# Softmax normalisation by eight pairs of ScalarE activations instead of two VectorE products

## What is computed

```python
s = jnp.einsum("bnqkgd,bnskd->bnkgqs", qb, kb) * (HEAD_DIM ** -0.5)
s = jnp.where(mask[None, :, None, None, :, :], s, NEG_INF)
m = jnp.maximum(jnp.max(s, axis=-1, keepdims=True), sink)
p = jnp.exp(s - m)
denom = jnp.sum(p, axis=-1, keepdims=True) + jnp.exp(sink - m)
o = jnp.einsum("bnkgqs,bnskd->bnqkgd", p / denom, vb)
```

## Time and profile before

| what | value |
|---|---|
| median of 3 runs | 2203.38 us (2201.78 to 2203.72) |
| profiled execution, its own time | 2202.2 us |
| span of the profiled execution | 2199.7 us |
| PE busy | 2152.1 us (98%) |
| DVE busy | 1655.6 us (75%) |
| ACT busy | 1209.2 us (55%) |

### The profile page before, as it was taken

How to read it: one execution, slowest core, us unless ns; L and a number is a source line. 1 busy time by engine, 2 the same in 40 slices (tenths; PEclk the granted TensorE clock), 3 DMA queues, 4 the chain that set the end, 5 groups by cost and what they waited for, 6 DMA issues and landing times.

```text
span 2199.7 us, 48658 instructions
## 1 busy us (share of the span) xinstructions
PE 2152.1 (98%) x19066; PEld 2092.8 (95%) x19066; DVE 1655.6 (75%) x2719; ACT 1209.2 (55%) x1838; POOL 0.5 (0%) x5
## 2 busy tenths in 40 slices
PE   8999999998999999999999999999999999999998
PEld 8988999998999999899999999999899999999998
DVE  7997877896858776787955777775678956877774
ACT  6555544555555445546646855445546647855443
POOL 0000000000000000000000000000000000000000
PEclk9999999999999999999999999999999999999999
DMA  7434565553345656564454356556554454455554
GB/s 244 146 125 127 178 205 189 174 182 116 126 157 187 211 185 200 179 189 144 163 174 143 127 190 203 190 185 206 184 177 146 162 177 131 137 193 186 185 188 134
DMA packets 102690, 376.57 MB, mean 171 GB/s; under 512 B 11520, under 2 KB 11648, under 8 KB 102016
## 3 DMA queue, kind: packets, MB, share of 16 engines
q1 hardware_dynamic: 101376, 368.67, 51.5%
q10 hardware_dynamic: 1152, 5.56, 0.7%
HBM read 373.14 MB, written 1.05 MB: 170 GB/s over the span
## 4 chain that ended last, share of the span: by engine, by line
PE 82%; DVE 12%; ACT 3%; issue 2%; DMA 0%; SPq 0%; DVEq 0%; ACTq 0%
PE acc L677 23%; PE acc L678 23%; PE acc L679 23%; DVE w_lo L1689 4%; PE acc L800 1%; PE acc L802 1%; PE acc L801 1%; ACT w_hi L1232 1%; PE mid L1134 1%; PE mid L1117 1%; PE mid L1032 1%; DVE pr L2424 0%; DVE branch L2175 0%; DVE zs L2056 0%; DVE prob L2091 0%
## 5 line engine op out<-in xcount | busy, mean ns | idle before, releaser
L1689 DVE TENSOR_TENSOR w_lo<-w_raw,w_hi 128x1024 fp32r<-128x1024 f32 x694 | 846.0, 1223 | 303.3 <-ACT w_hi L1232 295.4
L1232 ACT CAST w_hi<-w_raw 128x1024 fp32r<-128x1024 f32 x694 | 724.9, 1047 | 535.2 <-PE acc L679 490.2
L677 PE MATMUL acc<-h_hi,w_hi 128*128 128x256 f32 x2080 | 598.5, 288 | 8.7 <-DVE w_lo L1689 8.7
L678 PE MATMUL acc<-h_lo,w_hi 128*128 128x256 f32 x2080 | 586.6, 282 | 0.0
L679 PE MATMUL acc<-h_hi,w_lo 128*128 128x256 f32 x2080 | 583.3, 280 | 0.0
L677 PE MATMUL acc<-g_hi,w_hi 128*128 128x256 f32 x1488 | 421.4, 283 | 0.0
L678 PE MATMUL acc<-g_lo,w_hi 128*128 128x256 f32 x1488 | 416.6, 280 | 0.0
L679 PE MATMUL acc<-g_hi,w_lo 128*128 128x256 f32 x1488 | 416.4, 280 | 0.0
L677 PEld LDWEIGHTS acc<-h_hi,w_hi 128*128 128x128 f32 x2080 | 392.8, 189 | 16.8 <-DVE w_lo L1689 10.2
L678 PEld LDWEIGHTS acc<-h_lo,w_hi 128*128 128x128 f32 x2080 | 394.6, 190 | 0.5
L679 PEld LDWEIGHTS acc<-h_hi,w_lo 128*128 128x128 f32 x2080 | 394.9, 190 | 0.0
(11 more groups left out here) (447 smaller groups left out, 3414.1 us busy)
## 6 DMA issues: line engine op xcount, KB each, us to landing
w_raw<-weights_d SPq DMA_DIRECT2D x696, 512.0 KB, 3.5
p<-p_d ACTq DMA_DIRECT2D x3, 1080.0 KB, 8.4
rdec<-decay_d ACTq DMA_DIRECT2D x2, 768.0 KB, 6.6
p<-p_d SPq DMA_DIRECT2D x1, 1072.0 KB, 11.8
x<-x_d SPq DMA_DIRECT2D x2, 512.0 KB, 6.0
out_d<-work SPq DMA_DIRECT2D x4, 256.0 KB, 2.4
c<-c_d SPq DMA_DIRECT2D x1, 512.0 KB, 9.8
c<-c_d ACTq DMA_DIRECT2D x1, 448.0 KB, 10.5
```

The lines of the kernel that those rows point to most:

```text
L677: mm(dst, wh, hi[:, k, :], start=first and j == 0, stop=False)
L678: mm(dst, wh, lo[:, k, :], start=False, stop=False)
L1232: nc.scalar.copy(w_hi[:, slot, :], w_raw[:, slot, :]).then_inc(hi_done, 1)
L1689: tt(w_lo[:, slot, :], w_raw[:, slot, :], w_hi[:, slot, :].bitcast(F32), SUB).then_inc(lo_v, 1)
```

## The change

The two products leave DVE's `normalize`, which now ends with the reciprocals, written to a new small tile `rsum`. A new task `nrm` per head on ACT scales the head's two parts of `prob` in place by the reciprocals, with two Identity activations, and raises `a_p` once per head. In layer 0 heads 0 to 3 stand after slab 45 behind `gelu`, heads 4 to 7 after slab 46. In layer 1 heads 0 to 3 stand after slab 37 and heads 4 to 7 after slab 38. The transposes of each head wait for its own increment.

```diff
-        45: (("cx",), ("ssm_y",), ("normalize",), ("gelu",)),
-        46: (("gelu_lo",),),
+        45: (("cx",), ("ssm_y",), ("normalize",), ("gelu",), ("nrm", 0), ("nrm", 1), ("nrm", 2), ("nrm", 3)),
+        46: (("gelu_lo",), ("nrm", 4), ("nrm", 5), ("nrm", 6), ("nrm", 7)),
...
-        37: (("cx",), ("normalize",)),
-        38: (("ssm_y",),),
+        37: (("cx",), ("normalize",), ("nrm", 0), ("nrm", 1), ("nrm", 2), ("nrm", 3)),
+        38: (("ssm_y",), ("nrm", 4), ("nrm", 5), ("nrm", 6), ("nrm", 7)),
...
+        rsum = in_arena("rsum", 88000, [P, 2, HEADS])
...
                 if h < 2:
-                    pe.wait_ge(v_p, at.n + 1)
+                    pe.wait_ge(a_p, at.n * 8 + (h + 1))
                     if h == 1:
                         pe.wait_ge(v_yb, at.n * N1 + 2)
                 else:
+                    pe.wait_ge(a_p, at.n * 8 + (h + 1))
                     pe.wait_ge(a_pt, at.n * 8 + (h - 1))
...
+            def normalized(at, h):
+
+                act.wait_ge(v_norms, at.n + 1)
+                for r, (a, b) in enumerate(((0, P), (P, TRI))):
+                    last = nc.scalar.activation(prob[:, h, a:b], prob[:, h, a:b], ACT.Identity, scale=rsum[:, r, h:h + 1])
+                last.then_inc(a_p, 1)
...
                 tt(soft[:, 7, :, :], soft[:, 6, :, :], soft[:, 5, :, :], ADD).then_inc(dve_step, 1)
                 dve.wait_ge(dve_step, own.next())
-                nc.vector.reciprocal(soft[:, 8, :, :], soft[:, 7, :, :]).then_inc(dve_step, 1)
-                dve.wait_ge(dve_step, own.next())
-                for r, (a, b) in enumerate(((0, P), (P, TRI))):
-                    last = tt(prob[:, :, a:b], prob[:, :, a:b],
-                              soft[:, 8, r, :].unsqueeze(2).to_broadcast([P, HEADS, b - a]), MUL)
-                last.then_inc(v_p, 1)
+                nc.vector.reciprocal(rsum[:, :, :], soft[:, 7, :, :]).then_inc(v_norms, 1)
```

More of the change, by code:

```diff
@@ L505, in hybrid_kernel @@
         a_exp = sem("a_exp")
-        v_p = sem("v_p")
+        v_norms = sem("v_norms")
+        a_p = sem("a_p")
         pe_t = sem("pe_t")
@@ L1491, in _ @@
                         gelu(at)
+                    elif task[0] == "nrm":
+                        normalized(at, task[1])
                     elif task[0] == "pt_copy":
```

## The result

| | median us | against the kernel before |
|---|---|---|
| before | 2202.84 (8 runs) | |
| changed | 2208.25 (8 runs, 2205.73 to 2210.37) | 1.0026, 95% interval 1.0015 to 1.0037 |

The change makes the kernel 5.4 us slower by the medians (3.3 to 8.1 us by the interval); 5.1 us were forecast. The profiled execution of the changed kernel has a span of 2208.5 us, 8.8 us more than that of before. The rows show which part of it is the change.

What follows compares the result with a forecast made beforehand. PE was taken to bound the kernel (82% of the chain, DVE 12%). Terms 3.6 + 1.5 + 0 = +5.1 us on 2203.4 gave 2208.5 us, range 2204.5 to 2211.5.

Steps and rivals of the forecast that it cites:

- 3.6 us of waiting: Layer 0, before head 0's products: PE, ready at 194.11, waits for ACT's first copy, which ends at 197.7; +3.6 us.
- 1.5 us of clock: Layer 0, behind PE's new gap: a stretch of about 3.5 us at the lower clock, 1.2 GHz, costs +1.5 us.
- nothing in layer 1: Layer 1: ACT's idle gaps before the evictions of slabs 38, 39 and 40 hide the eight heads; 0 us.
- The room of 1.9 us: Layer 0: ACT's first copy ends near 192.2, PE wants it at 194.11; ACT has 1.9 us to spare.
- Nothing is gained on DVE: Removing DVE's two products, 3.43 us per layer, is credited nothing; in layer 0 DVE only waits longer for ACT's cast.
- the bounds are 0 and 1.6: Layer 0, behind PE's gap: the price of the lower clock lies between 0 and 1.6 us, from 3.5 us at 0.54.
- Rival A: Layer 0: the clock does not fall in the chain; only +3.6 us remains, 2207.0 us; chance 0.17.
- nothing but the copy is late: Layer 0: heads 0 and 1 and slab 49's rest are ready before PE wants them; only the first copy delays PE.
- B: Later gaps: stretches at half clock do not come again, each giving back 1.6 us; three make +0.3 us, 2203.7; chance 0.15.
- C's failing cover in layer 1: Layer 1: ACT's cover fails by 2.8 us, one of three ways to 2210 to 2211; chance 0.16 shared with the table load.
- E's table load: Layer 0: Identity behind the Sigmoid set brings a 1.28 us table load, 2209.8; chance 0.16 shared with the slower-still rival.
- D: Both layers: faster, if DVE's freed 3.43 us were on the path and ACT had more room; up to -6.9 us; chance 0.04.

Runs made afterwards that it cites:

- four pairs: Kernel before, VectorE's products kept, plus four pairs of Identity activations nobody waits for on ACT in layer 0: ratio 1.0007, +1.5 us.
- with eight: Kernel before, VectorE's products kept, plus eight pairs of Identity activations nobody waits for on ACT in layer 0: ratio 1.0028, +6.2 us.
- the kernel with the filled gap: Changed kernel plus eight unused matmuls of constants on PE ahead of head 0's products in layer 0: ratio 1.0013, +2.9 us against the kernel before.

## Why the prediction was right

The forecast was +5.1 us, made of 3.6 us of waiting, 1.5 us of clock and nothing in layer 1. The measured 5.4 us are made of the same parts and one of 0.37 us that the forecast did not have. That the totals agree within 0.3 us is in part luck: the interval goes from 3.3 to 8.1 us, and the clock's price differed by 0.7 us among three executions with the same gap.

*The first copy is what comes late.* It held to 0.04 us: 3.6 us were worked out, 3.56 us stand in the trace. A head costs 0.70 us where 0.69 us was taken, so the pair overlaps its neighbours as the rows of the Exp and of the long Identity said. The room of 1.9 us in ACT's queue, which the forecast subtracted, was tested by itself with four pairs (0.80 us of gap for 0.9 us expected) and with eight (3.56 us).

*Nothing is gained on DVE.* Behind the reciprocal DVE now idles 6.55 us until ACT's cast; before, it idled 0.34 us there. The row of the changed kernel:

```profile
195.08 1.23 DVE L1701 TENSOR_TENSOR w_lo<-w_raw,w_hi 128x1024 fp32r<-128x1024 f32 x1 [6.55 <-ACT w_hi L1235]
```

*The clock.* The mechanism was right. In the changed kernel the price, against the kernel with the filled gap, was 1.5 us, as taken. But the upper bound was too low: with the change in layer 0 alone the lower clock lasted longer than in the rows that the bound came from, and cost 2.25 us. The step that failed is "the bounds are 0 and 1.6": it took one stretch of 3.5 us for the longest that there is. Rival A (the clock does not fall) is refuted in the three executions profiled with that gap; its +3.6 us lie inside the interval of the times, so the traces decide this and the times do not.

*A small term was missed.* Even at full clock, head 0 to head 4 takes 6.75 us in place of 6.38 us. The sum 3.56 + 0.37 + 1.5 gives the 5.4 us. The forecast counted the first copy alone as late ("nothing but the copy is late"). Head 1's copy, 0.37 us behind it, is late too: where the first copy ends PE's wait, head 1's products start 0.37 us behind head 0's (196.14 and 196.52 with four added pairs) and no longer beside them (194.11 and 194.12 before). The 6.75 us are the same in both kernels that have a late copy at full clock, the one with four added pairs (202.89 - 196.14) and the one with the filled gap.

*Layer 1 hides its heads.* ACT was level again at slab 40's eviction, as predicted, and the change there alone measures 0.0 us.

*The rivals.* B (later stretches at the lower clock do not come again) is not seen in the changed kernel's trace, where the clock fell again behind the wait at 244.28 (0.51); for the executions without a trace it stays open. C's failing cover in layer 1 and E's table load are not in the trace: behind the table load of `gelu`'s end the Identities start without another. D is refuted: with the heads ahead of `gelu` ACT has room, DVE is rid of the products, and nothing is gained (+0.4 us).

The Trainium skill's rule that multiplications belong on VectorE ("ScalarE: Activation LUTs", section Rules for kernel authors) pointed the right way for the kernel as changed, but not for its reason. By engine time the trace agrees with it: eight heads take 2 x 2.79 = 5.58 us on ACT, where DVE took 3.43 us. But the loss is not that difference. With the same sixteen activations per layer ahead of `gelu` the difference is +0.4 us (-1.5 to +2.4), where engine time alone would have made it 4.1 us.

## What to carry to other kernels

That an engine is busy 55% of the time does not say whether it can take more work: look at the one place in its queue where the work will stand, measure the room between its last task there and the engine that waits for it, and subtract. Here eight heads of 0.70 us met 1.9 us of room, and the rest was the loss; 14 us earlier in the same queue the engine had idle time that hid it (no gap, +0.4 us, -1.5 to +2.4). When PE is made to wait, add a price for the lower clock behind the gap, and take it as a range from more than one row: behind gaps of 3.55 us the clock fell in three executions of three, for 1.5 to 2.25 us, and behind the one of 0.80 us it did not. And when the first of a pair of copies comes late, count the second one too.

## What the runs showed of the hardware that was not expected

The lower clock behind the same gap of 3.55 us came at different places: in the changed kernel's execution the granted clock was still 1.00 over the gap and 0.54 behind it, with the change in layer 0 alone it was 0.79 over the gap, 0.50 behind it and 0.71 over the 3.4 us after that, a difference of 0.7 us in what PE lost.

The products of two heads (128*64 in their rows) run side by side when both copies are there: 0.81 us for the pair, against 1.17 us when the second copy comes 0.37 us later.

PE's waits without a releaser in its streams of small matmuls differ by up to 3.5 us in all (8.2 to 11.7 us) among ten profiled executions, one of each kernel, though those streams are the same in all. The traces show what they may be: each of the 42 such waits of 0.9 us or more ends 2.2 to 2.9 us behind the start of a packet of 16 KB on the queue that the page lists as `q8 instruction`. Before the end of the wait at 184.72 in the changed kernel, it is the one such packet between 182.40 and 183.00 (packets, MB, share of 16 engines):

```profile
q8 instruction: 1, 0.02, 10.0%
```

So they look like waits for PE's own code to be loaded; no run tests that. The spread is more than half of what this change cost: two profiled spans, 8.8 us apart, would have given the wrong size; the starts of equal instructions give 5.4 us, as the medians do.
